# Expert rows gathered in shared sheets of 128, and all expert results summed to tokens on TensorE in turned form

## The chip, the cores and the metric

One core of a Trainium2 chip runs the whole program. The metric is device time in microseconds (us): the median of 3 runs is 936.79 us (936.52 to 938.85).

## The reference, cut to what matters

A decoder layer for 256 prompt tokens and 8 sample tokens (264 in all, width 1024). The mixer before the experts is not touched. Then

```python
scores = sigmoid(h @ router_w)                 # 64 experts in 8 groups
idx = top 8 experts of a token, out of the 4 best groups
w = scores[idx] / sum(scores[idx]) * 2.5       # gates, zero elsewhere
hg, hu = h @ e_gate[e], h @ e_up[e]            # 1024 -> 256, for each expert e
routed = sum_e (silu(hg) * hu * gate_e) @ e_down[e]     # 256 -> 1024
shared = (silu(h @ s_gate) * (h @ s_up)) @ s_down
x = x + gate2 * (routed + shared)
y = rmsnorm(x, final_g)
```

So there are 264 x 8 = 2112 pairs of a token and an expert, 33 for a mean expert. All arrays are float32.

## The kernel before, in words

Until about 350 us the mixer runs. Then 64 experts follow, each one *job*, sorted by how many tokens they have, in 16 groups of four (`UNROLL`). A job j of group i has a fixed number of row places: 128, 32, 64, 32 in a full group (`ROWS_OF_JOB`), 32, 64, 32, 64 in the two light groups 1 and 2, 128, 128, 32, 64 in group 0. Groups 6 to 14 are a hardware loop.

For each job these steps are done, on five engines that wait for each other by semaphores:

- SP loads the expert's three matrices, 1 MB each, into one of four slots (`reload`, L600 to L604). A slot is loaded again when the up-product of the job that held it is done (`up_done`).
- TensorE makes the list of a job's tokens from a one-hot (`token_list`, L1150), VectorE takes it over (`one_hot` L2112, `list_out` L2127, L2128), POOL gathers the rows of the job from `h_table` in device memory (`gather`, L759), TensorE turns them with eight transposes (`turn_rows`, helper line L856) into banks 5 and 6, ScalarE and VectorE copy one half each to `xgT` (`rows_out`, L1600, L2143).
- TensorE multiplies by gate and up (`up`, L1205 for 32 rows, L1208 for 128, L1210 and L1211 for 64), ScalarE applies silu (`gate_out`), VectorE multiplies by the gate (`gated`, L2162), TensorE turns the result (`turn_act`), ScalarE copies it (`act_out`), TensorE multiplies by `e_down` (`down`, L1236, L1245, L1250 and L1253) into banks 3 and 4.
- ScalarE copies bank 3 and VectorE bank 4 to `y_rows` (`y_out`, L1635, L2182), and POOL scatters the rows into the table `y_even` in device memory, with an addition (`scatter`, L771). Each scatter waits for the one before. POOL's order is: scatter of the job before, gather of the job three or four ahead.
- From group 5 on the largest job of a group (j = 0) isn't scattered: its result is split in a high and a low part (`y_high`, `y_low`), multiplied on TensorE by a 0/1 matrix `to_token` (`sum_rows`, L1269, 512 columns each), and VectorE multiplies the sums by gate2 and adds them to x (`add_sums`, L2225, L2227).

In the last group nothing is scattered: its results are gated (`gated_out`, L2195), kept in SBUF and summed on TensorE (`last_sum`, L1261), and the table is read back (L805), gated and added. TensorE's order within a job is written out in its `body`: first half of `up`, `turn_act` of the job before, second half, `turn_rows` of the next job, `down` of the job before, a list of the next group. In groups 3 and 4 six pieces of the shared expert stand behind jobs (L1172).

## Time and profile before

| | before |
|---|---|
| median of 3 runs | 936.79 us (936.52 to 938.85) |
| span of the profiled execution, first to last instruction | 933.8 us |
| TensorE matmuls busy | 858.9 us, 92% |
| VectorE busy | 562.4 us, 60% |
| ScalarE busy | 279.6 us, 30% |
| POOL busy | 157.5 us, 17% |
| moved by DMA | 302.75 MB, mean 324 GB/s |
| HBM written | 15.58 MB |

The time of the profiled execution itself isn't given apart; the runs lie 2.7 to 5.0 us over its span. Engines are PE (TensorE matmuls), PEld (its weight loads), DVE (VectorE), ACT (ScalarE), POOL, SP. A busy time of PE counts pipelined matmuls whose ends are modelled, so two neighbours overlap in the record: the distance of their starts is what one costs. PEclk is the granted TensorE clock as a share of 2.4 GHz. The DMA share is the mean busy share of the 16 transfer engines; 1.02 means busy without a break.

### The profile page before, as it was taken

To read this page: it belongs to the slowest core of one execution; us is meant where nothing else is said; L and a number is where in the kernel's file an instruction comes from. 1 tells how busy PE (TensorE), PEld (TensorE's weight loads), DVE (VectorE), ACT (ScalarE), POOL (GpSimd) and SP (SyncE) were. 2 spreads that over 40 slices of the span, in tenths; PEclk is the share of its full clock that TensorE was granted. 3 is DMA by queue.
4 is the path that set the end of the run, shared out by engine and by line. 5 is a ranking of instruction groups with operands and counts; after the bars stand their busy time and mean duration, and the time that the engine had idled before them with its cause. 6 is when DMAs were issued, how large, how long until landed. Compare 5 with 4: busy or idle time off the path is not lost.

```text
span 933.8 us, 21167 instructions
## 1 busy us (share of the span) xinstructions
PE 858.9 (92%) x7684; PEld 621.9 (67%) x7684; DVE 562.4 (60%) x1406; ACT 279.6 (30%) x535; POOL 157.5 (17%) x173
## 2 busy tenths in 40 slices
PE   4799999999999998997999998989999999999995
PEld 2699999999999897464555554545555555555551
DVE  2567988899986667243334435546546645645627
ACT  3554444444365240122211221212212212221223
POOL 2010000000000000123232323222222223213210
PEclk9899999999999998999899999999999999999998
DMA  9985558888776739799999999999999999999971
GB/s 341 331 242 163 177 178 287 269 281 280 266 250 242 240 107 390 305 387 391 399 387 392 387 381 384 414 391 396 413 397 384 411 399 387 405 395 387 404 267 64
DMA packets 98828, 302.75 MB, mean 324 GB/s; under 512 B 10314, under 2 KB 50378, under 8 KB 73780
## 3 DMA queue, kind: packets, MB, share of 16 engines
q1 hardware_dynamic: 88275, 281.63, 79.5%
q0 software_dynamic: 10000, 18.91, 6.9%
q10 hardware_dynamic: 489, 1.33, 0.4%
q8 instruction: 44, 0.72, 0.3%
q14 instruction: 20, 0.16, 0.0%
HBM read 300.61 MB, written 15.58 MB: 339 GB/s over the span
## 4 chain that ended last, share of the span: by engine, by line
PE 49%; DMA 40%; issue 4%; DVE 4%; ACT 1%; SPq 1%; POOLq 0%; DVEq 0%; ACTq 0%
DMA wexp<-in_e_up 31%; PE psum L852 28%; DMA y_even<-mT,scatter_row 6%; PE psum L1210 4%; PE psum L1208 3%; PE psum L856 3%; DMA xn<-h_table,idx 2%; PE psum L895 2%; DMA wexp<-in_ada_w 1%; PE psum L1245 1%; PE psum L1269 1%; PE psum L1096 1%; PE psum L1172 1%; PE psum L875 1%; PE psum L1205 1%
## 5 line engine op out<-in xcount | busy, mean ns | idle before, releaser
L852 PE MATMUL psum<-xn_r,wexp_r 128*128 128x264 f32 x1024 | 193.8, 288 | 5.9 <-DVE hT_r L1782 5.9
L852 PEld LDWEIGHTS psum<-xn_r,wexp_r 128*128 128x128 f32 x1024 | 161.7, 191 | 8.2 <-issue 7.8
L852 PE MATMUL psum<-hT_r,wexp_r 128*128 128x264 f32 x512 | 146.3, 286 | 0.0
L771 POOL DMA_INDIRECT y_even<-mT,scatter_row x50 | 72.4, 1447 | 303.1 <-DVE gcol L2128 140.6
L1744 DVE TENSOR_TENSOR wexp_r<-wexp,wexp_r 128x1024 fp32r<-128x1024 f32 x88 | 106.4, 1216 | 20.6 <-ACT wexp_r L1454 20.2
L1208 PE MATMUL psum<-wexp,mid 128*128 128x512 f32 x240 | 108.7, 598 | 10.0 <-DMA wexp<-in_e_up 8.4
L1454 ACT ACTIVATE wexp_r<-wexp 128x1024 fp32r<-128x1024 f32 x88 | 92.4, 1054 | 57.7 <-PE psum L852 44.4
L852 PEld LDWEIGHTS psum<-hT_r,wexp_r 128*128 128x128 f32 x512 | 97.8, 191 | 0.1
L2162 DVE SCALAR_TENSOR_TENSOR hT<-psum,gcol,hT 128x256 f32<-128x256 f32 (+2 forms) x64 | 26.2, 410 | 101.2 <-ACT hT L1616 100.9
L1208 PEld LDWEIGHTS psum<-wexp,mid 128*128 128x128 f32 x240 | 43.3, 190 | 61.6 <-issue 59.7
L852 PE MATMUL psum<-wexp_r 128*128 128x264 f32 (+2 forms) x576 | 82.4, 283 | 1.4 <-DVE wexp L1992 1.4
L1205 PE MATMUL psum<-wexp,mid 128*32 128x128 f32 x1984 | 70.0, 279 | 9.6 <-DMA wexp<-in_e_up 9.5
L852 PEld LDWEIGHTS psum<-wexp_r 128*128 128x128 f32 (+1 forms) x576 | 72.3, 177 | 4.2 <-issue 2.5
L1210 PE MATMUL psum<-wexp,mid 128*64 128x256 f32 x288 | 69.4, 384 | 6.1 <-DMA wexp<-in_e_up 6.1
L856 PEld LDWEIGHTS psum<-ident,xn 128*128 128x128 f32 (+1 forms) x432 | 54.3, 192 | 27.2 <-issue 15.4
L856 PE MATMUL psum<-ident,xn 128*128 128x128 f32 (+1 forms) x432 | 62.0, 288 | 10.5 <-DMA xn<-h_table,idx 7.9
L1211 PE MATMUL psum<-wexp,mid 128*64 128x256 f32 x288 | 69.8, 385 | 0.0
L759 POOL DMA_INDIRECT xn<-h_table,idx x48 | 52.3, 1091 | 98.5 <-DVE scatter_row L2136 54.6
L1608 ACT ACTIVATE hT<-psum 128x256 f32<-128x256 f32 (+2 forms) x64 | 17.7, 277 | 166.1 <-PE psum L856 165.9
L1205 PEld LDWEIGHTS psum<-wexp,mid 128*32 128x32 f32 x1984 | 53.1, 108 | 21.2 <-issue 17.3
L1245 PE MATMUL psum<-wexp,hT 128*128 128x512 f32 x120 | 54.0, 592 | 0.0
L1210 PEld LDWEIGHTS psum<-wexp,mid 128*64 128x64 f32 x288 | 36.7, 136 | 25.8 <-issue 12.8
(330 smaller groups left out, 1233.4 us busy)
## 6 DMA issues: line engine op xcount, KB each, us to landing
wexp<-in_e_gate SPq DMA_DIRECT2D x64, 1024.0 KB, 12.9
wexp<-in_e_up SPq DMA_DIRECT2D x64, 1024.0 KB, 26.1
wexp<-in_e_down SPq DMA_DIRECT2D x64, 1024.0 KB, 28.5
wexp<-in_w_in SPq DMA_DIRECT2D x32, 1024.0 KB, 6.1
mid<-in_ada_w SPq DMA_DIRECT2D x8, 2048.0 KB, 9.8
wexp<-in_w_branch SPq DMA_DIRECT2D x8, 1024.0 KB, 5.6
wexp<-in_ada_w SPq DMA_DIRECT2D x14, 512.0 KB, 10.6
wexp<-in_w_out SPq DMA_DIRECT2D x4, 1024.0 KB, 5.9
```

The source lines that it names most:

```text
L759: g.indirect_dma_start(out=xg[j][0:n], out_offset=None, in_=h_table, in_offset=bass.IndirectOffsetOnAxis(ap=idx[0:n, j, 0:1].bitcast(mybir ...
L771: g.indirect_dma_start(out=y_even, out_offset=bass.IndirectOffsetOnAxis(ap=scatter_row[0:n, j, :].bitcast(mybir.dt.uint32), axis=0), in_=y ...
L852: last = mm(out, a[x], b[y], start=start and x == y == 0, stop=stop and x == 1)
L856: return nc.tensor.transpose(out, src, ident[0:rows, 0:rows])
L1205: last = mm(psum[q * QUARTER:(q + 1) * QUARTER, j % 2, 0:P], x[:, k, 0:QUARTER], w[:, k, 1 - q // 2, q % 2:FE:2], start=(k == 0), stop=(k ...
L1208: last = mm(psum[:, j % 2, :].rearrange("p (a f) -> p a f", a=2), x[:, k, :], w[:, k], start=(k == 0), stop=(k == KT - 1))
L1210: mm(psum[HALF:CAP, j % 2, 0:FE], x[:, k, 0:HALF], w[:, k, 0], start=(k == 0), stop=(k == KT - 1), tile_position=(0, HALF))
L1211: last = mm(psum[0:HALF, j % 2, 0:FE], x[:, k, 0:HALF], w[:, k, 1], start=(k == 0), stop=(k == KT - 1), tile_position=(0, 0))
L1245: last = mm(psum[:, 3 + h, :], a[:, f, :], w[:, f, h * BLK:(h + 1) * BLK], start=(f == 0), stop=(f == 1))
L1454: F(as_r(high(u, q)), low(u, q), ACT.Copy).then_inc(S["w_hi"], 1)
L1744: V.tensor_tensor(as_r(low(u, q)), low(u, q), as_r(high(u, q)).bitcast(F32), ALU.subtract).then_inc(S["w_lo"], 1)
L2162: V.scalar_tensor_tensor(act[0:n, j % 2, 0:width], b, gcol[0:n, j, :], silu[0:n, j % 2, 0:width], ALU.mult, ALU.mult).then_inc(S["act_read ...
```

## The change

Only the expert stage changes.

- The row places of a group's jobs are laid side by side on *sheets* of 128 rows: two sheets a group (job 0 on one, jobs 1 to 3 on the other; in light groups two and two), three in group 0. POOL gathers a sheet at once and TensorE turns it at once; a job's `up` reads its columns of the turned sheet.
- The scatter, its table, the zeroing of the table, and the copy of the row numbers for it are gone. Every job's result goes to its rows of a sheet, split in high (ScalarE) and low (VectorE), both parts for all 1024 columns.
- The sums of a whole group are made in the next group, behind the up-product of job 1 (in group 0, of its own first two sheets, behind job 3): for each of eight blocks of 128 columns the sheets' high and low parts are the stationary operand and `to_token` (264 columns) the moving one, four matmuls into bank 5 or 6 in turn, and VectorE adds the block to an accumulator in turned form, `accT`. gate2 is applied once, in the last group, after TensorE has turned `accT` back.
- The lists of jobs 2 and 3 of the next group are both made in job 2, none in job 3.

The core of the diff (eight leading blanks and empty lines left out):

```diff
@@ -279,10 +276,9 @@
 tokid_i = sb("tokid_i", [P, 3], I32)
-idx = sb("idx", [P, UNROLL, 1], I32)
-scatter_row = sb("scatter_row", [P, UNROLL, 1], I32)
-gcol = sb("gcol", [P, UNROLL, 1])
-token_of = sb("token_of", [P, 2])
+idx = sb("idx", [P, 3, 1], I32)
+gcol = sb("gcol", [P, UNROLL + 1, 1])
...
-xg = [xn[:, 0, :], xn[:, 1, :], xn[:, 2, :], bc[:, 2, :]]
+xg = [xn[:, 0, :], xn[:, 1, :]]
+y_sheets = [(xn[:, 2, :], bc[:, 2, :]), (y_rows[:, 0, :], y_rows[:, 1, :])]
...
 token_order = in_mid(TOK)
+def place_of(i, j):
+    if first_group(i):
+        return ((0, 0), (1, 0), (2, HALF), (2, 0))[j]
+    if light_group(i):
+        return ((0, HALF), (0, 0), (1, HALF), (1, 0))[j]
+    return ((0, 0), (1, HALF), (1, 0), (1, HALF + QUARTER))[j]
...
+def sheet_of(i, s):
+    return s if first_group(i) else 2 * i + 1 + s
+def buffer_of(i, s):
+    return s % 2 if first_group(i) else 1 - s
+def next_sheet(i, j):
+    if j == UNROLL - 1:
+        return None if isinstance(i, int) and i == LAST else (i + 1, 0)
+    if first_group(i):
+        return ((0, 1), (0, 2), None)[j]
+    return (i, 1) if j == (1 if light_group(i) else 0) else None
...
+def sums_at(i, j):
+    return j == (UNROLL - 1 if first_group(i) else 1)
...
+    def gather(i, s):
+        lists = UNROLL * i + max(j for j in range(UNROLL) if place_of(i, j)[0] == s) + 1
+        at = buffer_of(i, s)
+        pool.wait_ge(S["lst_ready"], lists)
+        need(pool, S["xt_done"], sheet_of(i, s) - 1)
         pool.sem_inc(S["dma_may_go"], 1)
-        n = rows_used(i, j)
-        g.indirect_dma_start(out=xg[j][0:n], out_offset=None, in_=h_table,
-                             in_offset=bass.IndirectOffsetOnAxis(ap=idx[0:n, j, 0:1].bitcast(mybir.dt.uint32), axis=0),
-                             bounds_check=last_token, oob_is_err=False).then_inc(gathered[j], 16)
-    def scatter(i, j):
-        e = UNROLL * i + j
-        pool.wait_ge(S["scatter_row_ready"], e + 1)
-        need(pool, S["scattered"], 16 * scattered_before(i, j))
-        pool.wait_ge(S["ys_act"], e + 1)
-        pool.wait_ge(S["ys_dve"], e + 1)
-        pool.sem_inc(S["dma_may_go"], 1)
-        n = rows_used(i, j)
-        g.indirect_dma_start(out=y_even, out_offset=bass.IndirectOffsetOnAxis(ap=scatter_row[0:n, j, :].bitcast(mybir.dt.uint32), axis=0),
-                             in_=y_rows[0:n, j % 2, :], in_offset=None,
-                             bounds_check=last_token, oob_is_err=False, compute_op=ALU.add).then_inc(S["scattered"], 16)
+        g.indirect_dma_start(out=xg[at], out_offset=None, in_=h_table,
+                             in_offset=bass.IndirectOffsetOnAxis(ap=idx[:, s, 0:1].bitcast(mybir.dt.uint32), axis=0),
+                             bounds_check=last_token, oob_is_err=False).then_inc(gathered[at], 16)
...
+    def body(i):
+        for s in range(2):
+            gather(i + 1, s)
...
+    def turn_rows(i, s, sums):
+        g, at = sheet_of(i, s), buffer_of(i, s)
+        pe.wait_ge(gathered[at], 16 * (1 + s // 2 if first_group(i) else i + 1 + s))
+        need(pe, S["xgt_act"], g)
+        need(pe, S["xgt_dve"], g)
+        need(pe, S["sum_taken"], KT * sums)
+        for k in range(KT):
+            last = turn(psum[:, 5 + k // 4, (k % 4) * P:(k % 4 + 1) * P], xg[at][:, k:D:KT], P)
+        last.then_inc(S["xt_done"], 1)
...
+        s, at = place_of(i, j)
+        x, w = xgT[buffer_of(i, s)][:, :, at:at + rows_used(i, j)], w_gu[j]
...
+        in_last = isinstance(i, int) and i == LAST and j > 0
+        if in_last:
+            pe.wait_ge(S["ys_act"], 2 * UNROLL * LAST + j)
+            pe.wait_ge(S["ys_dve"], 2 * UNROLL * LAST + j)
+        else:
+            need(pe, S["ys_dve"], 2 * e - 1)
...
-    def sum_rows(i, t):
-        t0, n = TILES[t]
-        for h in range(2):
-            for y in (y_high, y_low):
-                last = mm(psum[0:n, 5 + h, :], as_r(to_token[:, 0, t0:t0 + n]), as_r(y[:, h * BLK:(h + 1) * BLK]),
-                          start=(y is y_high), stop=(y is y_low))
-        last.then_inc(S["sum_full"], 1)
...
+    def sums(i):
+        if first_group(i):
+            sheets, jobs, tokens = ((0, 0), (1, 1)), 2, 2
+        elif isinstance(i, int) and i == 1:
+            sheets, jobs, tokens = ((0, 0),), UNROLL, 3
+        else:
+            sheets, jobs, tokens = ((1, 0), (0, 1)), UNROLL * i, in_tokens(i - 1, 1)
+        pe.wait_ge(S["to_token_ready"], tokens)
+        pe.wait_ge(S["ys_dve"], 2 * jobs)
+        need(pe, S["sum_taken"], KT * i)
+        for c in range(KT):
+            if c > 1:
+                pe.wait_ge(S["sum_taken"], KT * i + c - 1)
+            for b, a in sheets:
+                for y in y_sheets[b]:
+                    last = mm(psum[:, 5 + c % 2, 0:TOK], as_r(y[:, c * P:(c + 1) * P]), as_r(to_token[:, a, :]),
+                              start=((b, a) == sheets[0] and y is y_sheets[b][0]), stop=((b, a) == sheets[-1] and y is y_sheets[b][1]))
+            last.then_inc(S["sum_full"], 1)
+    def turn_sums(t):
+        if t == 0:
+            pe.wait_ge(S["sum_taken"], KT * (LAST + 1))
+        else:
+            pe.wait_ge(S["acc_taken"], 1)
+        for c in range(KT):
+            last = turn(psum[:, 5 + c // 4, (c % 4) * P:(c % 4 + 1) * P], accT[:, c, t * P:(t + 1) * P], P)
+        last.then_inc(S["acc_turned"], 1)
...
+        pe.wait_ge(S["acc_taken"], 2)
         for h in range(2):
             last_sum(0, 0, h, first=True)
...
+        for c in range(KT):
+            p0 = SAMPLE_TILE * (c // 4)
+            mm(psum[p0:p0 + NS, SAMPLE_BANK, (c % 4) * P:(c % 4 + 1) * P], accT[:, c, SEQ:TOK], ident[:, :],
+               start=False, stop=False, tile_position=(0, p0))
...
-            if j == 0:
-                sums_taken(i, 0)
-            if j > 1 and is_summed(i, 0):
-                sums_taken(i, (3, 7)[j - 2])
-            if not (last and j == UNROLL - 1):
-                turn_rows(i if j < 3 else i + 1, (j + 1) % UNROLL)
+            if sums_at(i, j):
+                sums(i)
+            if next_sheet(i, j):
+                turn_rows(*next_sheet(i, j), sums_before(i, j))
+            if not last and j == 2:
+                token_list(i + 1, 2)
+            if last and j == 2:
+                turn_sums(1)
             if last and j == UNROLL - 1:
                 pe.wait_ge(S["act_ready"], NE - 1)
                 last_sum(0, 1, 0, first=True)
             if prev:
                 down(pi, pj)
-            if not last:
-                token_list(i + 1, j)
+            if not last and j < 3:
+                token_list(i + 1, (0, 1, 3)[j])
             if shared_piece_at(i, j) is not None:
                 shared_down(shared_piece_at(i, j))
-            if is_summed(i, 0):
-                sums_of_large(i, j)
+            if last and j == 1:
+                turn_sums(0)
             if last and j == 2:
                 first_sums_of_large()
...
+        n, rows = rows_used(i, j), rows_at(i, j)
+        high = y_sheets[buffer_of(i, place_of(i, j)[0])][0]
+        if not first_group(i):
+            ac.wait_ge(S["sum_full"], KT * (i + 1))
+        elif j > 1:
+            ac.wait_ge(S["sum_full"], KT)
+        for h in range(2):
+            ac.wait_ge(S["down_done"], 2 * e + 1 + h)
+            if n == QUARTER:
+                for q in (2 * h, 2 * h + 1):
+                    last = F(as_r(high[rows, q * FE:(q + 1) * FE]), psum[q * n:(q + 1) * n, 3 + h, 0:FE], ACT.Copy)
+            else:
+                p0 = CAP - n if h == 0 else 0
+                last = F(as_r(high[rows, h * BLK:(h + 1) * BLK]), psum[p0:p0 + n, 3 + h, :], ACT.Copy)
+            last.then_inc(S["ys_act"], 1)
...
+    def take_tokens(i):
+        ve.wait_ge(S["lst_ready"], UNROLL * i + UNROLL)
+        if not first_group(i):
+            ve.wait_ge(S["to_token_ready"], in_tokens(i - 1, 2 if isinstance(i, int) and i == 1 else 1))
+        n = 3 if first_group(i) else 2
+        V.tensor_copy(token_of[:, 0:n], idx[:, 0:n, :].rearrange("p s a -> p (s a)")).then_inc(S["token_taken"], 1)
+    def take_gate(i):
+        ve.wait_ge(S["lst_ready"], UNROLL * i + 2 * UNROLL)
+        ve.wait_ge(S["act_ready"], UNROLL * i + UNROLL)
+        V.tensor_copy(gcol[0:HALF, UNROLL - 1, :], gcol[0:HALF, UNROLL, :]).then_inc(S["gate_taken"], 1)
...
+        n, rows = rows_used(i, j), rows_at(i, j)
+        high, low = y_sheets[buffer_of(i, place_of(i, j)[0])]
+        for h in range(2):
+            ve.wait_ge(S["ys_act"], 2 * e + 1 + h)
+            if n == QUARTER:
+                parts = [(psum[q * n:(q + 1) * n, 3 + h, 0:FE], slice(q * FE, (q + 1) * FE)) for q in (2 * h, 2 * h + 1)]
+            else:
+                p0 = CAP - n if h == 0 else 0
+                parts = [(psum[p0:p0 + n, 3 + h, :], slice(h * BLK, (h + 1) * BLK))]
+            for whole, a in parts:
+                last = V.tensor_tensor(as_r(low[rows, a]), whole, as_r(high[rows, a]).bitcast(F32), ALU.subtract)
+            last.then_inc(S["ys_dve"], 1)
...
-    def large_to_tokens(i):
-        V.tensor_copy(token_of[:, 0:1], idx[:, 0, :]).then_inc(S["token_step"], 1)
-        ve.wait_ge(S["token_step"], sums_before(i) + 1)
-        V.tensor_scalar(as_r(to_token[:, 0, :]), token_order, token_of[:, 0:1], None, ALU.is_equal).then_inc(S["to_token_ready"], 1)
...
+    def add_sums(i):
+        for c in range(KT):
+            ve.wait_ge(S["sum_full"], KT * i + c + 1)
+            out = psum[:, 5 + c % 2, 0:TOK]
+            if first_group(i):
+                V.tensor_copy(accT[:, c, :], out).then_inc(S["sum_taken"], 1)
+            else:
+                V.tensor_tensor(accT[:, c, :], accT[:, c, :], out, ALU.add).then_inc(S["sum_taken"], 1)
...
+            link(V.tensor_tensor(sh_part[:], psum[:, 5 + h, :], bc[:, 3, a], ALU.mult))
+            if h:
+                ve.sem_inc(S["acc_taken"], 1)
+            link(V.tensor_tensor(x_sb[:, t, a], x_sb[:, t, a], sh_part[:], ALU.add))
...
-            if not last:
+            if j == 0:
+                take_tokens(i)
+            if not last and j < 3:
                 one_hot(i + 1, j)
-            if not last:
-                keep_scatter_row(i, j)
-            elif j == 0:
-                rows_to_tokens()
-            if is_summed(i, j):
-                large_to_tokens(i)
-            if is_summed(i, 0) and j == 2:
-                add_sums(i, 2)
+            if not last and j == 2:
+                one_hot(i + 1, 3)
             gated(i, j)
-            if not (last and j == UNROLL - 1):
-                rows_out(i if j < 3 else i + 1, (j + 1) % UNROLL)
-            if last and j == UNROLL - 1:
-                gate_table(1)
+            if not last and j == UNROLL - 1:
+                take_gate(i)
+            if first and j == 1:
+                ve.wait_ge(S["tokens_in"], 1)
+                link(V.tensor_copy(token_order, token_order.bitcast(I32)))
+                for s in range(2):
+                    sheet_to_tokens(i, s)
+            if sums_at(i, j):
+                add_sums(i)
+            if first and j == UNROLL - 1:
+                sheet_to_tokens(i, 2)
+            if not first and j == 2:
+                for s in range(2):
+                    sheet_to_tokens(i, s, rounded=not last)
+            if next_sheet(i, j):
+                rows_out(*next_sheet(i, j))
+            if first and j == 0:
+                ve.wait_ge(S["token_taken"], 1)
+                rows_unused(0)
+                link(rows_unused(1))
+            if not last and j == 2:
+                list_out(i + 1, 2)
             if last and j:
                 gated_out(pj)
             elif prev:
-                y_out(pi, pj)
-            if last and j == UNROLL - 1:
-                add_table(1)
-            if not last:
-                list_out(i + 1, j)
+                y_out(i if j else i - 1, pj)
+            if not last and j < 3:
+                list_out(i + 1, (0, 1, 3)[j])
             if shared_piece_at(i, j) is not None:
                 take_shared(shared_piece_at(i, j))
-            if is_summed(i, 0) and j > 1:
-                add_sums(i, j - 2)
-            if last and j == 2:
-                gate_table(0)
-                add_table(0)
+            if last and 0 < j < 3:
+                add_turned(j - 1)
```

## Rows read from the trace of the kernel before

**Rows 1.** The page: the span, and part 1, busy time of each engine.
```profile
span 933.8 us, 21167 instructions
...
PE 858.9 (92%) x7684; PEld 621.9 (67%) x7684; DVE 562.4 (60%) x1406; ACT 279.6 (30%) x535; POOL 157.5 (17%) x173
```
**Rows 2.** Stretches of 50 us: busy us of each engine, PEclk, DMA share, GB/s.
```profile
400.00:450.00 50.00, 42.76 (x456) 26.93 (x457) 17.17 (x70) 10.36 (x30) 13.74 (x13) 0.93 1.01 388
...
500.00:550.00 50.00, 49.87 (x453) 27.53 (x449) 20.27 (x64) 10.06 (x28) 12.22 (x11) 1.00 1.02 381
...
600.00:650.00 50.00, 46.52 (x410) 26.65 (x403) 29.67 (x80) 9.97 (x26) 14.07 (x11) 1.00 1.02 398
650.00:700.00 50.00, 46.00 (x430) 27.12 (x430) 25.52 (x75) 11.12 (x29) 12.16 (x10) 1.00 1.01 403
```
**Rows 3.** Waits, 600 to 850 us: waiter <- waited for: us, times, longest.
```profile
PE psum L1205 <- DMA wexp<-in_e_up: 6.6, 8, 1.0
PE psum L1208 <- DMA wexp<-in_e_up: 6.0, 8, 1.3
PE psum L1210 <- DMA wexp<-in_e_up: 4.1, 7, 0.7
...
POOL y_even L771 <- DMA y_even<-mT,scatter_row: 33.3, 8, 4.8
```
**Rows 4.** Timeline of TensorE: first up-matmul of groups 1 to 6 and 15.
```profile
410.66 0.32 PE L1205 MATMUL psum<-wexp,mid 128*32 128x128 f32 x4
...
436.70 0.32 PE L1205 MATMUL psum<-wexp,mid 128*32 128x128 f32 x4
...
469.58 0.70 PE L1208 MATMUL psum<-wexp,mid 128*128 128x512 f32 x1
...
506.35 0.59 PE L1208 MATMUL psum<-wexp,mid 128*128 128x512 f32 x1
...
538.05 1.12 PE L1208 MATMUL psum<-wexp,mid 128*128 128x512 f32 x2
...
574.77 0.69 PE L1208 MATMUL psum<-wexp,mid 128*128 128x512 f32 x1 [1.38 <-DMA wexp<-in_e_up]
...
883.16 0.67 PE L1208 MATMUL psum<-wexp,mid 128*128 128x512 f32 x1 [1.01 <-DMA wexp<-in_e_up]
```
**Rows 5.** Waits of TensorE, 405 to 475 us.
```profile
PE psum L856 <- DMA xn<-h_table,idx: 6.4, 2, 4.8
PE psum L856 <- DMA bc<-h_table,idx: 2.5, 1, 2.5
```
**Rows 6.** DMA queues, 355 to 901 us: packets, MB, share of 16 engines.
```profile
q0 software_dynamic: 8560, 13.91, 9.4%
```
**Rows 7.** The same, 625.2 to 626.5 us.
```profile
q0 software_dynamic: 47, 0.07, 26.6%
```
**Rows 8.** The same, 626.5 to 628.9 us.
```profile
q0 software_dynamic: 90, 0.28, 29.1%
```
**Rows 9.** Timeline of TensorE: split products, turned rows, sums of a large job.
```profile
207.40 4.77 PE L852 MATMUL psum<-wexp_r 128*128 128x264 f32 x38
...
639.06 1.15 PE L856 MATMUL psum<-ident,xn 128*128 128x128 f32 x8
...
663.92 1.09 PE L1269 MATMUL psum<-mod_room_r,hT_r 128*8 128x512 f32 x4
```
**Rows 10.** Groups by shape: count, busy us, mean ns, idle before, releasers.
```profile
L2227 DVE TENSOR_TENSOR x_sb<-x_sb,mod_room 128x512 f32<-128x512 f32 x40 | 27.7, 692 | 1.4
...
L2182 DVE COPY mT<-psum 32x256 f32<-32x256 f32 x58 | 24.5, 422 | 35.0 <-PE psum L1236 19.1 <-DMA y_even<-mT,scatter_row 15.4
...
L1635 ACT ACTIVATE mT<-psum 32x256 f32<-32x256 f32 x58 | 21.7, 375 | 34.8 <-PE psum L1236 19.0 <-DMA y_even<-mT,scatter_row 15.5
```
**Rows 11.** A short stretch, columns as in rows 2.
```profile
444.00:450.00 6.00, 5.92 (x21) 2.70 (x23) 0.69 (x2) 0.69 (x2) 0.28 (x1) 0.52 1.02 399
```
**Rows 12.** DMA issues: count, median us from issue to landing.
```profile
xn<-h_table,idx POOLq DMA_INDIRECT x48, 7.7
```

## What the change was expected to do

> **What bounds the kernel now.** I read the head of the page first (span 933.8 us, TensorE busy 858.9 us of it [rows 1]), then a table by stretches of 50 us [rows 2]. From 400 us on, where the experts run, the DMA share is 1.01 to 1.02 in every stretch: the transfer engines never rest. TensorE rests a little (46.52 of 50 us at 600 to 650) but not at 500 to 550 (49.87 of 50). The list of waits for 600 to 850 us says for what: TensorE waits 6.6 + 6.0 + 4.1 = 16.7 us for expert weights and for nothing else of that size [rows 3], 2.3 us in each group of four experts. So the late groups go by the weights. The early ones don't: between 410 and 574 us no wait for weights shows until the 1.38 us before 574.77 [rows 4]; TensorE waits for gathered rows (8.9 us between 405 and 475, the longest 4.8 [rows 5]), because POOL issues scatters and gathers in one order and each scatter waits for the one before (33.3 us of such waits between 600 and 850 [rows 3]).
>
> The starts of the groups give the periods [rows 4]. Group 1 takes 436.70 - 410.66 = 26.04 us, group 2 32.88, group 3 36.77 (four pieces of the shared expert in it), group 4 31.70, group 5 36.72, and groups 6 to 14 take (883.16 - 574.77)/9 = 34.27 each. Without the 2.3 us of waits a late group holds 32.0 us of TensorE work. After 883.16 come 50.6 us of last group, sums and output.
>
> **What the change takes from the DMA engines.** Between 355 and 901 us the software queue moves 13.91 MB [rows 6], 3396 rows of 4 KB. 2112 are gathers (264 tokens, 8 experts each), 128 the load of final_g; the other 1156 are scattered rows. The price of one I read from two short stretches. In the one that holds scattered rows alone the queue takes 26.6% of 1.3 us for 0.07 MB, 17 rows: 0.346/17 = 20.3 ns a row [rows 7]. In the one with gathered rows alone it takes 29.1% of 2.4 us for 0.28 MB, 68 rows: 10.3 ns [rows 8]. The gathers stay, row for row. The scatters' 1156 x 20.3 ns = 23.5 us go. That is what the weight stream can gain, 1.4 to 1.5 us in a late group, whose floor falls from 34.3 to 32.8 us. The table that is no longer zeroed (1 MB) and read back at the end falls into other work: zero taken, 3 us at most.
>
> **What it adds to TensorE.** Per group:
> - Eight transposes for each sheet instead of for each job: two batches fewer. A batch takes 1.15 us [rows 9], its end beside the next matmul; I take 1.1: -2.2 us (group 0, three sheets: -1.1).
> - The old sums, in groups 5 to 14 alone: three batches of four 512-wide matmuls, 1.09 us each [rows 9]: -3.3 us.
> - The new sums, in every group from 0 to 13 and again in 14 and the last (16 times): eight column blocks of four matmuls of 264 columns. 38 of that kind take 4.77 us [rows 9], 0.121 us apart, so 32 x 0.121 = 3.9 us if nothing holds them. But only banks 5 and 6 are used in turn, and VectorE must add each block first. 128x512 takes 0.692 us there and the 32x256 copy 0.422 [rows 10]: about 0.43 for 264 columns. One bank's round is then 0.48 (four matmuls) + 0.16 (end of the last) + 0.43 + 0.1 (two hand-overs, my estimate from neighbouring starts) = 1.17 us for two blocks, 0.58 a block: 4.7 us for eight. VectorE reaches the first block some 0.3 us late, since it has y_out, list_out, a one-hot and `gated` before it. I take 5.0. Bounds: 3.9 and 9.3 (each block waits for the one before it, 8 x 1.17).
> - In groups 0 to 2 the turn of the next sheet stands behind the sums in banks 5 and 6: +0.65 us for the last block's addition.
> - The lists of jobs 2 and 3 are both made in job 2. The second waits for list_out of the first, which VectorE reaches only after two one-hots, `gated` (0.47) and two token tables (0.36 each): about 2.2 us after the last up-product, while TensorE has 1.2 us to do (a list, a small down). +1.0 us; bounds 0 and 2.
>
> Full groups without sums before: -2.2 + 5.0 + 1.0 = +3.8. The light groups 1 and 2: +4.4. Late groups: -2.2 - 3.3 + 5.0 + 1.0 = +0.5, so 32.5 us. Group 0: -1.1 + 5.65 = +4.6.
>
> **VectorE and ScalarE.** y_out becomes a chain: ScalarE copies a half to high, VectorE subtracts it to low, for both halves, where each engine did one half. VectorE gains 2.4 us of subtractions a group, and eight additions of 0.43 replace twelve of 0.68; it is busy 29.67 of 50 us at 600 to 650 [rows 2], and 20.27 at 500 to 550, where it gains 6 us a group. As a sum that costs nothing. As a chain it matters before `sums`, which wait for the y_out of the group's last job: 0.76 + 0.86 + 0.86 us (pairs of the 0.375 and 0.422 us operations [rows 10]) behind its down-product, while TensorE has a list and the quarter job's 2.5 us of up-products: just hidden; the cover is 0.2 us thin.
>
> **POOL.** Seven indirect issues in a late group become two, and none waits for a scatter. A sheet's gather is issued when its last list is out and then has 9 us or more; in the kernel before, gathers land 7.7 us after issue [rows 12]. The 8.9 us of gather waits of groups 1 and 2 go. So does the lower clock behind the longest: after TensorE has idled 4.8 us the granted clock is 0.52 from 444 to 450 [rows 5, 11], the 1.2 GHz level, and 5.9 us of busy time there would be 3.1 at 2.4 GHz: 2.8 us.
>
> **The sum along TensorE.** Group 1 starts at 410.66 + 4.6 = 415.2. Group 2: 26.04 - 2.5 + 4.4 = 27.9, at 443.1. Group 3: 32.88 - 6.4 - 2.8 + 4.4 = 28.1, at 471.2. Group 4: + 36.77 + 3.8, at 511.8. Group 5: + 31.70 + 3.8, at 547.3. Ten groups of 32.5: the last group starts at 872.3, where it was 883.16. The weights alone would allow 883.16 - 23.5 = 859.7, so TensorE is now the later one throughout: of 23.5 us freed 10.9 are used.
>
> **The end.** In the last group there are now the sums of group 14 (+4.5, VectorE being free sooner), two fewer batches of turned rows (-2.2), no waits for weights (-1.4), two batches that turn the accumulator back (+2.2), and eight small matmuls for the samples (+1.0). The 512-wide first sums wait until VectorE has emptied banks 5 and 6 of the second turned part: behind the gates of job 1 (1.7 us), a product, a sum and a product of 0.69 each: TensorE stands 4.0 us; what stood there before was 0.4. Together +7.6 (bounds +3 and +12). 872.3 + 50.6 + 7.6 = 930.5 us of span, 3.3 less than 933.8. The median shown is 936.79, 3.0 over the span; that part lies outside the span and I keep it: 936.8 - 3.3 = 933.5, say 933.
>
> **Rivals.**
> 1. *The weight stream stays the bound.* For it: the DMA share over 1.0, and the only waits of the late groups are for weights. Against: a late group has only 2.3 us of slack and the change adds work. It needs the sums near 3.9 and no wait for lists: 872.3 gives way to 859.7, and the end is 12.6 us earlier: 921. The Trainium skill's rule speaks for this case ("Perfetto Trace Analysis", section Identifying the Most-Contended Engine: find the most contended resource, by HBM utilization for DMA, and optimize that one first). By that rule the whole 23.5 us would be earned.
> 2. *Slower: the hand-overs hold TensorE.* One mechanism: all of y_out now passes ScalarE, then VectorE, then frees banks 3 and 4 and the sheets for `down` and `sums`, and the sums themselves alternate with VectorE's additions. For it: VectorE's order puts one-hots and lists between them, and my cover is 0.2 us. Each 0.1 us more per group costs 1.5 us over 15 groups; from 0.25 us the gain is gone, from 0.45 it is slower than the bound below. At 1 us: 948.
> 3. *The sheets come late.* A sheet waits for the last of its three lists. If its gather then needs 1 us more than it has in 14 groups: 947. Against: without scatters ahead gathers should land sooner.
> 4. *The clock.* The short stops in the sums could lower it; a half clock for 6 us in each group would cost 3 us each, 975. Against it: with stops of about 1 us in every late group the stretches at 600 to 700 show 1.00 [rows 2]. The Trainium skill has this case ("TensorE: Matmul & The Clock Gate", section A second HAM failure mode: psum-queue depth-cycling: cycling through banks with short idles can make the clock fall again and again). No run of before shows it for stops so short.
>
> **How the numbers follow.** Forecast 0.45 (its own range 926 to 940: 0.45 us either way in a late group and the bounds of the end), rival 1 0.22 (921), rival 2 0.23 (948), rival 3 0.07, rival 4 0.03. The range of 8 in 10 is 920 to 947. A difference of 0.3%, 2.8 us, is about what a measurement of this kernel can tell. Faster (under 934.0): all of rival 1 and 0.6 of the forecast, 0.49. Same: 0.3 of the forecast and the near ends of 2 and 3, 0.21. Slower: 0.30.
>
> **What would show it.** The scatters gone and the software queue near half its share; no wait of TensorE for weights after group 3; the 32 matmuls of a group's sums taking 4.7 to 5.2 us with VectorE between them; a stop of about 1 us before the last list of a group; group periods of 32.5; the last group starting at 872; a stop of 4 us ahead of the first 512-wide sums. Wrong it would be if weights are still waited for in late groups, if the sums take over 6 us, or if `sums` or `down` wait for y_out.

## The result, and the profile after

The kernel after takes 947.64 us (median of 4 runs, 945.86 to 949.04); the kernel before took 937.18 us beside it (936.52 to 938.85). The ratio is 1.0103, 95% interval 1.0087 to 1.0118: the change makes the kernel slower, by 1.0%. The forecast was 933.

The page of the kernel after, its head and the chain that ended last:

```profile
span 945.6 us, 21235 instructions
...
PE 874.9 (93%) x7840; PEld 646.9 (68%) x7840; DVE 577.9 (61%) x1447; ACT 308.3 (33%) x583; POOL 50.1 (5%) x89
...
PE 78%; DVE 10%; issue 4%; DMA 4%; ACT 3%; SPq 0%; DVEq 0%; ACTq 0%; POOLq 0%
```

Against [rows 1] TensorE is busy 16 us more and the span is 11.8 us longer. The same line of the kernel before:

```profile
PE 49%; DMA 40%; issue 4%; DVE 4%; ACT 1%; SPq 1%; POOLq 0%; DVEq 0%; ACTq 0%
```

In its chain DMA held 40%; here it holds 4%. What the change was to remove is gone. DMA queues from 355 to 901 us, and the issues with the median us to landing:

```profile
q0 software_dynamic: 4896, 9.19, 4.5%
...
wexp<-in_e_gate SPq DMA_DIRECT2D x62, 1024.0 KB, 7.7
wexp<-in_e_up SPq DMA_DIRECT2D x62, 1024.0 KB, 9.9
wexp<-in_e_down SPq DMA_DIRECT2D x62, 1024.0 KB, 10.2
```

The software queue moves 9.19 MB where it moved 13.91 [rows 6]. TensorE's waits from 355 to 946 us, and then only those from 600 to 850, the stretch of [rows 3]:

```profile
PE psum L1158 <- DVE gcol L2141: 11.5, 12, 1.0
PE psum L1293 <- DVE mid L2242: 5.2, 14, 0.6
PE psum L1274 <- DVEq L2251: 4.2, 1, 4.2
...
PE psum L864 <- DMA xn<-h_table,idx: 2.0, 1, 2.0
PE psum L1274 <- ACT mod_room L1659: 1.9, 1, 1.9
...
PE psum L1263 <- DVE bc_r L2200: 0.7, 2, 0.3
```
```profile
PE psum L1158 <- DVE gcol L2141: 7.8, 8, 1.0
PE psum L1293 <- DVE mid L2242: 3.3, 8, 0.4
```

No wait for weights is left. Line 1158 is a list of tokens, 1293 the new sums, 1274 the 512-wide sums of the end, 864 the turn of gathered rows. The largest waits are for VectorE. Stretches of 50 us (busy us of PE, PEld, DVE, ACT, POOL; granted clock; DMA share; GB/s):

```profile
400.00:450.00 50.00, 43.44 (x481) 28.50 (x473) 28.01 (x88) 13.06 (x33) 4.22 (x4) 1.00 0.96 376
500.00:550.00 50.00, 47.19 (x402) 25.78 (x400) 29.14 (x78) 11.68 (x29) 2.99 (x2) 1.00 0.78 302
600.00:650.00 50.00, 46.99 (x445) 30.08 (x447) 27.35 (x83) 12.55 (x31) 2.99 (x3) 1.00 0.99 398
```

At 500 to 550 the transfer engines stand a fifth of the time (share 0.78, 1.02 before [rows 2]): slots for weights come free too slowly. SyncE, which issues the loads, waits 39.4 of these 50 us for TensorE's products, 32.0 before. The bound has changed hands, from the weights to TensorE and what it waits for. First up-matmul of groups 1 to 6 and of the last:

```profile
417.94 0.52 PE L1211 MATMUL psum<-wexp,mid 128*32 128x128 f32 x9
...
448.54 0.63 PE L1211 MATMUL psum<-wexp,mid 128*32 128x128 f32 x13
...
477.44 0.70 PE L1214 MATMUL psum<-wexp,mid 128*128 128x512 f32 x1
...
518.09 0.59 PE L1214 MATMUL psum<-wexp,mid 128*128 128x512 f32 x1
...
554.62 0.70 PE L1214 MATMUL psum<-wexp,mid 128*128 128x512 f32 x1
...
587.82 0.70 PE L1214 MATMUL psum<-wexp,mid 128*128 128x512 f32 x1
...
882.70 0.70 PE L1214 MATMUL psum<-wexp,mid 128*128 128x512 f32 x1
```

Group 1 starts 7.3 us later than in [rows 4], group 5 16.6 us later. Then 32.8 us a group win back against 34.3, and the last group starts 0.5 us earlier than before (882.70, 883.16). The end, 62.9 us instead of 50.6, makes the loss.

### The profile page after: what moved, and what is told of

Same layout as the page of the kernel before. It is cut to its first block, busy times and chain, and to the rows that moved or that the text cites. A ratio compares the mean times of both kernels' runs of the same rounds, so it can differ in the third digit from the quotient of the medians.

```text
span 945.6 us, 21235 instructions
## 1 busy us (share of the span) xinstructions
PE 874.9 (93%) x7840; PEld 646.9 (68%) x7840; DVE 577.9 (61%) x1447; ACT 308.3 (33%) x583; POOL 50.1 (5%) x89
## 4 chain that ended last, share of the span: by engine, by line
PE 78%; DVE 10%; issue 4%; DMA 4%; ACT 3%; SPq 0%; DVEq 0%; ACTq 0%; POOLq 0%
PE psum L860 26%; PE psum L1214 11%; PE psum L1293 6%; PE psum L864 6%; PE psum L1257 5%; PE psum L1216 5%; PE psum L1211 4%; PE psum L1263 3%; PE psum L1248 2%; PE psum L903 2%; DMA wexp<-in_ada_w 1%; DVE bc_r L2200 1%; DMA wexp<-in_w_in 1%; PE psum L1217 1%; PE psum L1158 1%
## 5 line engine op out<-in xcount | busy, mean ns | idle before, releaser
L2200 DVE TENSOR_TENSOR bc_r<-psum,xn_r 32x256 fp32r<-32x256 f32 (+2 forms) x140 | 67.6, 483 | 46.3 <-ACT xn_r L1645 27.1
L2242 DVE TENSOR_TENSOR mid<-mid,psum 128x264 f32<-128x264 f32 x120 | 50.0, 426 | 20.4 <-PE psum L1293 17.9
L792 POOL DMA_INDIRECT xn<-h_table,idx x33 | 34.6, 1049 | 490.9 <-DVE gcol L2141 461.0
L1293 PE MATMUL psum<-hT_r,mT_r 128*128 128x264 f32 x240 | 54.7, 309 | 5.7 <-DVE mid L2242 4.2
L1628 ACT ACTIVATE hT<-psum 128x256 f32<-128x256 f32 (+2 forms) x64 | 21.1, 329 | 102.7 <-PE psum L1214 52.3
L1620 ACT ACTIVATE hT<-psum 128x256 f32<-128x256 f32 (+2 forms) x64 | 17.6, 276 | 110.8 <-PE psum L864 110.6
## 6 DMA issues: line engine op xcount, KB each, us to landing
wexp<-in_e_down SPq DMA_DIRECT2D x64, 1024.0 KB, 10.2
```

The costliest lines, as they stand in the source:

```text
L1293: last = mm(psum[:, 5 + c % 2, 0:TOK], as_r(y[:, c * P:(c + 1) * P]), as_r(to_token[:, a, :]), start=((b, a) == sheets[0] and y is y_sheet ...
L2200: last = V.tensor_tensor(as_r(low[rows, a]), whole, as_r(high[rows, a]).bitcast(F32), ALU.subtract)
L2242: V.tensor_tensor(accT[:, c, :], accT[:, c, :], out, ALU.add).then_inc(S["sum_taken"], 1)
```

## The experiments

The kernel before took 936.9 to 937.4 us beside all of them. "Both moves" below is `e5_both`. The edits are shown shortened; "..." stands for what is left out. e1, e2, e6 and e7 leave part of the result out.

| label | what | us | ratio to before (95%) |
|---|---|---|---|
| e1_no_sums | after, sums left out | 899.81 | 0.9592 (0.9571 to 0.9614) |
| e2_before_no_scatter | before, scatters left out | 909.75 | 0.9708 (0.9681 to 0.9735) |
| e6_high_only | after, half the sums' matmuls | 938.75 | 1.0015 (0.9993 to 1.0036) |
| e7_no_adds | after, no additions | 929.08 | 0.9896 (0.9863 to 0.9929) |
| e3_lists | after, last list later | 934.18 | 0.9966 (0.9952 to 0.9980) |
| e4_tail | after, first sums of the end later | 940.09 | 1.0035 (1.0017 to 1.0053) |
| e5_both | e3 and e4 | 926.89 | 0.9885 (0.9870 to 0.9899) |
| e11_after_banks | after, sums over three banks | 929.97 | 0.9917 (0.9903 to 0.9931) |
| e8_banks | three banks and both moves | 910.78 | 0.9722 (0.9709 to 0.9735) |
| e10_light | both moves, earlier list in light groups | 924.91 | 0.9870 (0.9855 to 0.9884) |
| e9_banks_light | all of these | 905.57 | 0.9663 (0.9650 to 0.9675) |

**What the scatters cost, and what the weights allow.** The first experiment takes the new work away, the second takes the old transfers away from the old kernel.

```
 e1:  def sums(i):         +  if not first_group(i): pe.sem_inc(S["sum_full"], KT); return
      def add_sums(i):     +  if not first_group(i): wait sum_full ...; ve.sem_inc(S["sum_taken"], KT); return
 e2:  def scatter(i, j):   -  pool.sem_inc(S["dma_may_go"], 1)
                           -  g.indirect_dma_start(out=y_even, ... compute_op=ALU.add).then_inc(S["scattered"], 16)
                           +  pool.sem_inc(S["scattered"], 16)
```

> The kernel after, without the 32 matmuls of the sums and VectorE's eight additions in every group but the first (so those results are left out); every wait stays. My theory: after the change TensorE sets the time throughout, and the sums cost it 5.0 us a group. Then groups 1 to 5 shorten by about 5 us each until the weight stream is met, the last group starts near 860 us (883.16 less the 23.5 us of scatters; it is at 882.7 in the kernel after), a late group keeps 32.8 us but now with waits for weights, and the time is near 920. Rival: the weight stream bounds the kernel after as well (its DMA share is 0.98 to 1.00 in the late groups). Then the last group still starts at 880 to 883 and only the sums of the tail are saved: 941 to 943.

> The kernel before, with the scatter's DMA left out (its waits and its signal stay, so 1156 rows are not added to the tokens). My theory: the scatters cost the weight stream 20.3 ns a row, and the kernel before is bound by that stream: the late groups fall from 34.3 us to TensorE's own 32.0 to 32.8, and groups 1 and 2 lose most of their 8.9 us of waits for gathered rows; time 912 to 918, so the change took away what it should and TensorE spent it again. Rival: the scatters' packets lie in gaps of the weight stream, and what they cost is their order on the software queue alone: late groups stay at 34.1 to 34.3, and only groups 1 and 2 gain: 927 to 932.

Measured 899.81 and 909.75, both below what I had expected. Start of the last group in the kernel without sums, its waits of TensorE from 600 to 850 us, and its stretch 600 to 650; then the start of the last group of the kernel before without scatters:

```profile
842.97 0.67 PE L1214 MATMUL psum<-wexp,mid 128*128 128x512 f32 x1 [1.13 <-DMA wexp<-in_e_up]
```
```profile
PE psum L1211 <- DMA wexp<-in_e_up: 8.7, 6, 2.1
PE psum L1214 <- DMA wexp<-in_e_up: 8.6, 7, 2.1
```
```profile
600.00:650.00 50.00, 44.33 (x483) 26.70 (x482) 24.40 (x77) 15.60 (x39) 3.99 (x4) 0.97 1.02 421
```
```profile
856.28 0.59 PE L1204 MATMUL psum<-wexp,mid 128*128 128x512 f32 x1
```

With the sums gone the waits for weights are back, 17.3 us of them: here the stream is the bound, and it lets the last group start at 843. My bound of 859.7 was 17 us too late. Its pace fits the bytes: the stream runs at 421 GB/s, and twelve weights of 1024 KB with some 130 gathered rows are 13.1 MB a group, 31.2 us. In the kernel before it ran at 398 to 403 GB/s [rows 2].

The scatters are only a part of that difference. Without them, from the start of group 9 (659.08) to that of the last (856.28), the kernel before takes 32.9 us a group, where it took 34.2 with them: 1.3 us less, against the 1.4 to 1.5 that the price of 20.3 ns a row had given. From 650 to 850 us, the kernel before, and then the same without scatters:

```profile
650.00:850.00 200.00, 185.26 (x1704) 108.68 (x1703) 113.82 (x311) 43.28 (x113) 51.04 (x41) 1.00 1.01 399
```
```profile
650.00:850.00 200.00, 192.88 (x1753) 113.96 (x1756) 117.41 (x325) 44.44 (x117) 24.79 (x24) 0.99 1.02 408
```

Without scatters it still moves only 408 GB/s, at nearly the same DMA share as the kernel without sums with its 420. Neither of these two has scatters; they differ in the gathers (four a group against two sheets) and in all the rest of the change, and no run takes these apart. So the change gave the stream a second gain, some 13 us by the start of the last group (856.28 to 842.97), which my bound had at nothing, and its cause stays open.

The kernel before gained 27 us by leaving the scatters out, in late groups and in the waits for gathers of the early ones. The rival (transfers in gaps, 927 to 932) falls, and so does "the weights bound the kernel after". All of the gain, and 10 us more, went into TensorE's time.

**What the sums cost.** One kernel halves the matmuls, the other leaves the additions out.

```
 e6:  -  for y in y_sheets[b]:                 +  for y in y_sheets[b][:1]:            ... (and stop= at the last sheet)
 e7:  -  V.tensor_tensor(accT[:, c, :], accT[:, c, :], out, ALU.add).then_inc(S["sum_taken"], 1)
      +  ve.sem_inc(S["sum_taken"], 1)
```

> The kernel after with the sums over the high parts alone: 16 matmuls of 264 columns instead of 32, the additions as they are (the low parts are left out of the result). If the number of matmuls sets the sums, they take half, 2.5 us a group less, and the last group starts where the weights allow, near 862: about 922. If VectorE's additions in two banks set them (0.43 us each, and the hand-overs: (0.24 + 0.16 + 0.43 + 0.1)/2 = 0.47 a block, 3.7 us for eight), they fall from 5.0 to 3.7 only, 1.3 us a group: 928 to 930.

> The kernel after with all 32 matmuls of the sums, but VectorE only signals and does not add after the first group (so the later groups' sums are left out of the result). The matmuls then go at their own pace, 32 x 0.121 = 3.9 us instead of 5.1: if my theory of the sums is right (matmuls 3.9, the rest hand-overs), 1.2 us a group less in 15 groups, 18 us: 929. If the matmuls' own pace sets all of it, the time stays at 946 to 948.

Measured 938.75 and 929.08. VectorE's additions and some of TensorE's matmuls in one late group of the kernel after (start, us, engine, operation, idle before and its releaser):

```profile
633.50 0.75 DVE L2242 TENSOR_TENSOR mid<-mid,psum 128x264 f32<-128x264 f32 x2
634.75 0.92 DVE L2242 TENSOR_TENSOR mid<-mid,psum 128x264 f32<-128x264 f32 x2 [0.50 <-PE psum L1293]
636.03 0.91 DVE L2242 TENSOR_TENSOR mid<-mid,psum 128x264 f32<-128x264 f32 x2 [0.36 <-PE psum L1293]
637.30 0.91 DVE L2242 TENSOR_TENSOR mid<-mid,psum 128x264 f32<-128x264 f32 x2 [0.36 <-PE psum L1293]
```
```profile
632.32 0.51 PE L1293 MATMUL psum<-hT_r,mT_r 128*128 128x264 f32 x2
...
633.96 0.51 PE L1293 MATMUL psum<-hT_r,mT_r 128*128 128x264 f32 x2 [0.41 <-DVE mid L2242]
...
635.24 0.51 PE L1293 MATMUL psum<-hT_r,mT_r 128*128 128x264 f32 x2
...
637.46 0.29 PE L1293 MATMUL psum<-hT_r,bc_r 128*128 128x264 f32 x1
```

Both engines wait for each other: a round of two blocks takes 1.27 us (634.75, 636.03, 637.30), 0.64 a block, where four matmuls need 0.48 and the addition 0.43. Without the additions a late group takes (866.27 - 582.78)/9 = 31.5 us against 32.8, so the hand-over costs 1.3 us a group. With half the matmuls the round is still 1.03 us (additions start at 628.57, 629.60 and 630.63): 0.9 us a group less, not 2.5. So the round through two banks is what counts, not the number of matmuls alone. 15 groups of 0.9 would give 13 us; e6 came out 9 us under the kernel after, and I had expected 18 or more. In part the clock eats the rest. Its stretches from 754 us:

```profile
754.00:757.00 3.00, 1.94 (x11) 1.42 (x11) 2.59 (x10) 0.28 (x1) 1.00 (x1) 1.00 0.99 415
757.00:760.00 3.00, 2.82 (x9) 1.61 (x9) 1.63 (x4) 0.00 (x0) 0.00 (x0) 0.71 1.01 426
760.00:763.00 3.00, 3.00 (x6) 1.25 (x5) 0.45 (x1) 0.60 (x1) 0.00 (x0) 0.72 1.02 425
```

During sums in which TensorE is busy only 1.94 of 3 us the granted clock is still 1.00; in part of the next 6 us it is at the 1.2 GHz level, and that group takes 33.6 instead of 31.9. It happened in two late groups of this execution, some 3.3 us together. The sums alone don't set it: the same stretch a group earlier, 722 to 725 us, also has 1.94 of 3 us, and behind it the clock stays at 1.00 (722 to 725, 725 to 728):

```profile
722.00:725.00 3.00, 1.94 (x14) 1.44 (x10) 2.68 (x10) 0.28 (x1) 1.00 (x1) 1.00 0.99 407
725.00:728.00 3.00, 2.82 (x12) 1.71 (x11) 1.55 (x4) 0.00 (x0) 0.00 (x0) 1.00 1.01 423
```

What made the difference is not shown. The ten executions of this kernel lie between 934.9 and 942.3 us, the three slowest with a mean clock of 0.972 to 0.976, the three fastest with 0.980 to 0.984. This is rival 4, in two groups. The Trainium skill's page "TensorE: Matmul & The Clock Gate" has it under A second HAM failure mode: psum-queue depth-cycling (short idles between groups of matmuls that cycle through banks make the clock go back and forth). The trace agrees with half the matmuls, in two groups of ten, and shows nothing of it with the full number: there the clock stays at 1.00.

**The two stops.** The last list of the next group moves into job 3; the first sums of the end move behind the down-product of job 2.

```
 e3, PE:   up(i, j, range(4))
        +  if not last and j == 3: token_list(i + 1, 3)         (and no longer behind down in job 2)
     DVE:  +  if not last and j == 3: list_out(i + 1, 3)        (ahead of gated(i, j))
 e4, PE:-  if last and j == 2: first_sums_of_large()
        +  if last and j == 3: first_sums_of_large()            (behind down(i, 2))
        +  rows_ready(1); pe.wait_ge(S["to_token_ready"], ...)  (ahead of last_sum in job 3)
```

> The kernel after with one part moved: the last list of the next group is made in the middle of the up-products of job 3, where VectorE has long put out the list before it, and not behind the down-product in job 2. My theory (TensorE bounds the kernel after, and stands 0.97 us a group ahead of that list; 1.0 was forecast): 0.9 to 1.0 us less in each of some 14 groups, 13 us; time 934 to 936, late groups 31.9 us or 32.8 where the weights then bind. Rival, the weight stream is already the bound in the late groups: the wait goes and comes back as a wait for weights, 0 to 3 us less: 944 to 948. Rival, VectorE is what is late, so that the stop moves to the next place where TensorE meets it (sums or turned rows): within 2 us of the kernel after.

> The kernel after with one part moved in the last group: the first 512-wide sums and the samples' eight small matmuls stand behind the down-product of job 2, in job 3, and not ahead of its up-products, so that TensorE does job 3's up-products while VectorE empties the banks. The tail is off TensorE's critical path nowhere: the 4.2 us stop goes, and if the stop is what lets the clock fall to half (0.57 granted from 914 to 921), the 2.9 us of slow matmuls too: 7 us less, 940. If the clock falls for another reason, 4 us less: 943. Rival, the end waits for VectorE's chain or job 3's weights anyway: 946 to 948.

> The kernel after with both moves: the last list in the middle of job 3's up-products, and the first 512-wide sums of the end behind the down-product of job 2. If TensorE is the bound in both places the gains add: 13 + 7 = 20 us less, 927 to 929, which is below both kernels. If the late groups meet the weight stream: 935 to 937, no better than the kernel before.

Measured 934.18, 940.09 and 926.89, each within 0.2 us of the range forecast from TensorE's time. What the end looks like in the kernel after: the stop, the sums behind it, and the stretch:

```profile
908.88 1.07 PE L1248 MATMUL psum<-wexp,hT 128*32 128x256 f32 x16
914.17 3.75 PE L1274 MATMUL psum<-mT,hT 128*128 128x512 f32 x4 [4.21 <-DVEq L2251]
917.85 1.88 PE L1274 MATMUL psum<-mod_room,hT 128*8 128x512 f32 x4
```
```profile
914.00:921.00 7.00, 6.83 (x29) 2.63 (x33) 0.69 (x1) 0.00 (x0) 0.00 (x0) 0.57 0.00 0
```

And the same stretch in `e4_tail`, where TensorE does job 3's up-products while VectorE empties the banks:

```profile
905.00:914.00 9.00, 9.00 (x100) 5.64 (x99) 5.66 (x11) 2.15 (x6) 0.00 (x0) 1.00 0.00 1
914.00:921.00 7.00, 7.00 (x57) 2.82 (x53) 5.48 (x10) 2.49 (x6) 0.00 (x0) 1.00 0.01 2
```

The stop was 4.2 us, and with it went the half clock behind it: from the start of the last group to the end of the span `e4_tail` takes 55.2 us (941.1 - 885.95), the kernel after 62.9. In `e3_lists` the wait at line 1158 for `gcol` is gone, and a late group takes 31.67 us. The gains add: `e5_both` is 20.8 us under the kernel after and 1.1% under the kernel before; the list alone already brings the change below the kernel before, by 0.3%.

**Three banks.** If TensorE may be two blocks ahead, neither engine waits.

```
 -  if c > 1:  pe.wait_ge(S["sum_taken"], KT * i + c - 1)
 +  if c == 2: pe.wait_ge(S["actT_ready"], ...)                  (bank 2 free of the turned activation)
 +  if c > 2:  pe.wait_ge(S["sum_taken"], KT * i + c - 2)
 -  psum[:, 5 + c % 2, 0:TOK]        +  psum[:, (5, 6, 2)[c % 3], 0:TOK]       (PE and DVE)
 +  pe.wait_ge(S["sum_taken"], ...)  (ahead of turn_act and shared_down, which use bank 2)
```

> The kernel after with one part changed: the sums go round three banks (5, 6 and 2) instead of two, so that TensorE may be two blocks ahead of VectorE's addition. Without the additions a late group took 31.5 us, with them 32.8, so the hand-over costs 1.3 us a group. If it is the two banks that make this cost, and not VectorE's pace (0.43 us a block against 0.48 of four matmuls), nearly all of it goes: 31.6 us a group, 15 to 19 us less in all, 929 to 932. Rival, VectorE's pace: it adds a block in 0.43 and has a hand-over of 0.1 to 0.2 of its own, so it stays the later one: 0 to 0.4 us a group, 942 to 947.

> The same three banks on the kernel that has both moves (926.9 us, TensorE the bound with 31.66 us a late group). If the weight stream has room (without the sums its last group started at 843, here it starts at 871), the gain of 1.2 us a group comes through: late groups 30.4 to 30.6 us, 909 to 912. Rival, the weights' pace of 31.5 us a group binds as soon as TensorE is faster, since the stream was never more than one group ahead: 920 to 925, with waits for weights in the late groups.

Measured 929.97 and 910.78. VectorE in a late group of `e11_after_banks`:

```profile
629.00 2.37 DVE L2247 TENSOR_TENSOR mid<-mid,psum 128x264 f32<-128x264 f32 x5 [0.17 <-PE psum L1295]
```

Five additions in 2.37 us, 0.47 each: the pace of four matmuls. The kernel is 17.7 us faster by that alone, as fast as with no additions at all (929.08). VectorE's pace is not what the sums cost; the two banks are. On top of both moves the gain is 16.1 us, so the weight stream had the room.

**A list in the light groups.** In groups 1 and 2 the next first sheet waits for list 1, which stood behind a down-product and a y_out.

```
 +  early = light_group(i) and j == 1         (and "not early" at the old place ...)
 +  if early: token_list(i + 1, 1)    (PE, ahead of down)       if early: list_out(i + 1, 1)   (DVE, ahead of y_out)
```

> The kernel with both moves, and in the two light groups the second list of the next group ahead of the down-product and of VectorE's y_out, so that the gather of the next group's first sheet is issued some 2 us earlier. TensorE waits 2.85 us for that sheet at 444.5 us (2.0 in the kernel after). If the issue time is what is late, 2 us less: 925. If the gather's landing, 8 us under a full stream, takes what it is given, or the list then waits for VectorE: 926 to 927, no difference that shows.

> Three banks, both moves and the earlier list in the light groups. If each is TensorE's time the gains add: 907 to 910. If the weight stream binds: as the kernel with three banks and both moves, within 1 us.

Measured 924.91 and 905.57: 2.0 us and 5.2 us less; the second is below my range of 907 to 910. Of the wait for the sheet (2.85 us in `e5_both`, 2.7 in `e8_banks`) nothing is left in the first and 0.2 us in the second. Where the second kernel found more than that wait is not settled: its profiled execution also reached the experts 1.6 us earlier than that of `e8_banks` (374.8, 376.4), with a better clock at 360 to 371 us (0.84, 0.69). `e9_banks_light` is the best kernel here, 3.4% faster than before. Its head and two stretches:

```profile
PE 854.1 (95%) x7840; PEld 640.0 (71%) x7840; DVE 577.2 (64%) x1447; ACT 308.3 (34%) x583; POOL 50.4 (6%) x89
```
```profile
600.00:650.00 50.00, 49.89 (x477) 31.77 (x470) 27.45 (x81) 14.67 (x36) 3.99 (x4) 1.00 1.02 421
650.00:700.00 50.00, 49.80 (x454) 30.40 (x453) 27.38 (x83) 14.83 (x36) 2.99 (x3) 1.00 1.01 420
```

TensorE is busy all the time, and the transfer engines too: here the two bounds meet. From 600 to 850 us no wait of TensorE is left in the list.

## Why the prediction was wrong

Its mechanism stood: the gain of the stream is real, TensorE becomes the later engine throughout, and it decides. Its sum came to a span of 930.5; the span was 945.6. The step that failed is "The sum along TensorE" with "The end": the terms were right in kind and too small in size, and every row of the table has the same sign. The largest miss is the end, where the stop stood in the sum and the half clock behind it did not.

| part | forecast | measured | miss |
|---|---|---|---|
| before the experts | as before (375.7) | 377.7 | +2.0 |
| group 0 | +4.6 | 40.25 - 34.97 = +5.3 | +0.7 |
| group 1 | 27.9 | 30.6 | +2.7 |
| group 2 | 28.1 | 28.9 | +0.8 |
| groups 3 and 4 | 40.6, 35.5 | 40.65, 36.5 | +1.1 |
| groups 5 to 14 | 32.5 each | (882.70 - 554.62)/10 = 32.8 | +3.1 |
| the end | 58.2 | 62.9 | +4.7 |

- *Before the experts.* Not shown to be of the change: in the stretch 360 to 371 us the granted clock was 0.53 here, 0.69 before, but the kernels of the experiments, whose code is the same up to there as that of the kernel after, reached the experts anywhere from 374.8 to 378.2. One execution can't tell 2 us here.
- *Group 1.* "The gather waits of groups 1 and 2 go" was wrong for one sheet. POOL waits for nothing but its list, as said, but the list itself is late: its VectorE step stands behind y_out. 2.0 us, and `e10_light` got them. The other 0.7 us is not taken apart.
- *The late groups.* The sums were forecast at 5.0 us. A round of two blocks took 1.27 against my 1.17, and in the shown group the sums take 5.27 us, from 632.32 to the start of the next matmul (637.59). The wait for the list is 0.97 (forecast 1.0). That seems to account for the 0.3 a group, but two more errors lie under it. My 32.0 us of TensorE's work in a late group was the period less the listed waits; without scatters, in groups 5 to 8, where no weight is waited for, the kernel before takes 31.45. So the change added 1.3 us to a late group where I had +0.5, and that the period was off by only 0.3 is partly luck. I also took the three old batches of sums at the length of their records, 3.3 us; by the distance of starts they cost 3.1. I had the cost of the sums and its cause and did not see that it could be bought off for nothing.
- *The end.* The stop was 4.2 us (forecast 4.0). The half clock behind it, 2.9 us, was not in the sum, though the prediction had read it off the kernel before (4.8 us of rest, then 0.52 [rows 5, 11]). The wait for ScalarE before the second sums grew from 1.0 to 1.9 us, which was missing too. Some 0.6 us of the miss is left without a cause. The terms that the prediction lists give +7.7, not +7.6.
- *Outside the span* lay 1.7 us in the execution of the kernel after (947.34 - 945.6), not 3.0: 1.3 us the other way. Every execution with both numbers on record has 1.7 to 1.9, so the 3.0 was no cost outside the span: the profiled execution of the kernel before was a quick one. That is also why the spans differ by 11.8 us and the medians by 10.5.

Rival 1 (weights stay the bound, 921) fell; the rule of the Trainium skill that I had quoted for it ("Perfetto Trace Analysis", Identifying the Most-Contended Engine) named the bound of the kernel before rightly: `e2_before_no_scatter` is 27 us faster, where 23.5 was the whole of it by that rival. But the change also loads the engine that stood 2.3 us behind. The weight bound of 859.7 that rival and sum share was too late by 17 us. Rival 2 (hand-overs, 948) has the number, but only half the mechanism: `sums` never wait for y_out, and `down` does so twice, 0.7 us in all, in groups 1 and 2 (L1263 for L2200 in the list of 355 to 946 us); the alternation of sums and additions is the part that held. Its price list stood in the prediction: from 0.25 us a group the gain is gone. The late groups had 0.3, and I gave the case 0.23. Rival 3 (late sheets) held once, for 2 us. Rival 4 was not seen in the groups of the kernel after; its half clock came in the end, behind a long stop and not behind short ones. Two readings of the prediction were off, without weight for the sum: TensorE waited 0.7 us for weights at 565.50 already, before the 1.38 at 574.77, and the DMA share from 400 us on is 1.00 to 1.02 up to 850 us and 0.94 behind, not 1.01 to 1.02 in every stretch.

## What to carry to other kernels

When the next engine stands 2.3 us behind the bound in a period of 34 (2.8 by the kernel without scatters), work taken from the bound is worth that distance and not more, and each wait that the change adds to the next engine counts in full. Measure the next engine's own period by a run that takes the bound's work away, not by subtracting waits. Price the hand-overs of the new work as rounds (matmuls, end, read, two signals) over the number of banks, and ask for a third bank before anything else: here it was worth 17.7 us, more than the change lost. A stop of about 4 us of TensorE costs its own length and a half clock behind it; put work there that waits for nothing.

## What the runs showed of the hardware

- A scattered row with addition took 20.3 ns of all 16 transfer engines where a gathered row took 10.3, both 4 KB [rows 7, 8]. Leaving the scatters out brought a late group from 34.2 to 32.9 us, about what that price gives, and let the stream run at 408 GB/s instead of 399 (both from 650 to 850 us).
- A DMA share of 1.01 does not say that the stream is at its best: it was 1.01 to 1.02 at 398 GB/s, at 408 and at 421.
- In the kernel after, where slots came free late, the weights land in 7.7 to 10.2 us (median). They took 20 to 25 us in `e2_before_no_scatter` and 18 to 24 in `e1_no_sums`, where the stream was waited for. It is a sign and no proof: in the late groups of the kernel before, bound by the stream, from 600 to 850 us, `e_gate` landed in 12.1 us while `e_up` took 26.2.
- The clock fell in two of ten late groups with half the matmuls in the sums, and in none with all of them; it cost up to 1.7 us in a group. Why in these two is not shown. In `e1_no_sums`, with waits for weights of up to 2.1 us, the stretches of 50 us from 600 to 850 show a granted clock of 0.90 to 0.97.
